# Dealing the rows of a down unit to partitions in neighbouring pairs

## The chip, the cores and the metric

The kernel runs on one core of a Trainium2 chip. The metric is the time of one execution on the device in microseconds; several executions are timed and the median is told. A profiled execution gives the trace.

## The reference

One layer of a decoder for 256 tokens of width 1024, in float32: a mixer (pooling and attention), and then a mixture of experts, which takes nearly all of the time. Of the experts this matters:

```python
for e in range(N_EXPERTS):                       # 32
    gu = jnp.dot(t, w_gu[e]) + b_gu[e]           # t (256, 1024), w_gu[e] (1024, 2048)
    gate = jnp.minimum(gu[:, :D_EXPERT], 7.0)
    lin = jnp.clip(gu[:, D_EXPERT:], -7.0, 7.0)
    act = gate * jax.nn.sigmoid(1.702 * gate) * (lin + 1.0)
    y = jnp.dot(act, w_down[e]) + b_down[e]      # w_down[e] (1024, 1024)
    out = out + combine[:, e:e + 1] * y          # top 4 of 32 experts
```

The weights of the experts are 256 MiB (`w_gu`) and 128 MiB (`w_down`), and each is read once.

## The kernel before

**Units.** The experts' weights come through `raw`, a ring of 12 slots (`RAW`) of 1 MB, each 128 partitions of 8 KB. A unit fills one slot with one DMA. An expert has 8 units of `w_gu` ("gu units") and 4 of `w_down` ("down units"). Gu unit `c` holds the 128 rows `128c` to `128c+127` of `w_gu[e]`, one row of 2048 floats on each partition. Down unit `u` holds the 256 rows `256u` to `256u+255` of `w_down[e]`, two rows of 1024 floats on each partition: partition `p` gets the rows `256u+p` and `256u+128+p`.

**The loading queue.** SyncE issues all units in a fixed order, in `load` (line 296 for gu units, line 302 for down units), after a wait on `unit_used`, which TensorE raises when it has done its last matmul on a unit; so a slot is loaded again as soon as the unit 12 places back is used. The semaphore `raw_loaded` of the slot says that it has landed. The first 12 gu units are issued before the loop over the experts starts.

**TensorE.** The loop runs over pairs of experts, 24 units a pair, 16 pairs. `gu_unit` and `down_unit` multiply up to 64 gathered tokens of the expert by the unit: 8 matmuls of 512 columns each, on the two column halves of the array by turns. In `gu_unit` the tokens lie in `xT`, in `down_unit` in `actT`, and the matmul for block `m = 2u + r` of the hidden channels pairs `actT[:, half, m, :]` with the 1024 floats `raw[:, slot, r*1024:...]`. Partition `p` of block `m` must hold the same hidden channel in both. `mm` is a helper, so all matmuls have line 817.

**From gu to actT.** When the 8 gu units of an expert are done, ScalarE copies the result from PSUM to `gu` (tokens on partitions, line 504), `turn_gu` transposes it in eight 128x128 blocks (line 1035; `gu` is the operand that is loaded as weights or streamed against an identity), VectorE clips both halves (lines 756 and 757) and, with ScalarE's sigmoid (line 509), writes `actT` (line 763). Block `m` of the transpose becomes block `m` of `actT`, channel `128m + p` on partition `p`. Between the units TensorE also does the scatter of the expert before, the gather for the next pair (`gather`), transposes of the dispatch masks (line 1085) and the biases.

**The end.** The last pair's final eight units are all down units; between the second and the third of the last four TensorE does `last_scatter(0)`, after the fourth `last_scatter(1)`; then come the sums into `acc`, the final norm and the store.

Of the kernel before, what the change touches and what calls it, by code (L numbers as in the profile page):

```python
# [25 lines left out]
P = 128  # L26
# [59 lines left out]
def hybrid_layer(nc, x, g_mix, w_in, w_pool, pool_scale, w_out, g_ffn, w_router, b_router,  # L86
                 w_gu, b_gu, w_down, b_down, g_final, consts, out):
    KB = 1024
    with ExitStack() as ctx:
        def sem(name):  # L90
            return ctx.enter_context(nc.semaphore(name))
# [6 lines left out]
        def at(name, shape, dt, off):  # L98
            size = 4
            for s in shape[1:]:  # L100
                size *= s
            assert off + size <= arena_bytes, (name, off, size)
            return nc.alloc_sbuf_tensor_at(name, shape, dt, offset=base + off)

        raw = at("raw", [P, RAW, UW], F32, 0)
        h2 = at("h2", [P, TT, D], F32, 96 * KB)
        gu = at("gu", [P, FE], F32, 128 * KB)
# [97 lines left out]
        def c_(name, rows=P):  # L205
            lo, hi = _AT[name]
            return cst[0:rows, lo:hi]
# [7 lines left out]
        raw_loaded = [sem(f"raw_loaded{s}") for s in range(RAW)]  # L215
# [42 lines left out]
        def pair_of(i):  # L258

            return i % PAIRS  # L260
# [9 lines left out]
        @block.sync  # L270
        def _(sp):
            for t in range(TT):
                sp.dma_start(acc[:, t, :], x[0, t * P:(t + 1) * P, :]).then_inc(x_loaded[t], 16)
            sp.dma_start(cst[:], consts).then_inc(const_loaded, 16)
            for c in range(DC):
                sp.dma_start(raw[:, c, :], w_in[0, c * P:(c + 1) * P, :]).then_inc(raw_loaded[c], 16)
            sp.dma_start(wpool[:], w_pool[0].rearrange("g c d -> c g d")).then_inc(wpool_loaded, 16)
            for b in range(2):
                for h in range(2):
                    sp.dma_start(bgu[b * E:(b + 1) * E, h, :],  # L280
                                 b_gu[0, :, h * FE + b * 512:h * FE + (b + 1) * 512]).then_inc(bgu_loaded, 16)

            sp.dma_start(wout[:], w_out[0].rearrange("(c p) n -> p c n", p=P)).then_inc(wout_loaded, 16)
            sp.dma_start(wrt[:], w_router[0].rearrange("(c p) e -> p c e", p=P)).then_inc(router_loaded, 16)
            sp.dma_start(brt[:], b_router.broadcast_to([P, E])).then_inc(router_loaded, 16)
            sp.dma_start(gffn[:], g_ffn.broadcast_to([P, D])).then_inc(gffn_loaded, 16)
            sp.wait_ge(ysc_zeroed, 1)
            for h in range(2):
                sp.dma_start(ysc[h * SLOTS:h * SLOTS + E, 0, :], b_down[0, :, h * 512:(h + 1) * 512]).then_inc(bdown_loaded, 16)

            def load(e, first, slot_unit):

                s = slot_unit % RAW
                if first < GU_U:
                    src = w_gu[0, bass.ds(e, 1), first * P:(first + 1) * P, :].rearrange("a p n -> p (a n)")
                    sp.dma_start(raw[:, s, :], src).then_inc(raw_loaded[s], 16)  # L296
                else:
                    u = first - GU_U
                    src = w_down[0, bass.ds(e, 1), 2 * u * P:2 * (u + 1) * P, :].rearrange(
                        "a (r p) n -> p (a r) n", p=P)  # L300
                    dst = raw[:, s, :].rearrange("p (r n) -> p r n", r=2)
                    sp.dma_start(dst, src).then_inc(raw_loaded[s], 16)  # L302

            for c in range(PRE_U):
                sp.wait_ge(win_low, c + 1)
                load(0, c, c)
            sp.wait_ge(projected, 3)
            for k in range(EARLY):
                load(1, k, PRE_U + k)
            sp.wait_ge(rounds_ready, 1)  # L310
            last_pair = sp.snap(sp.value_load(further[0:1, 0:1], min_val=0, max_val=T // SLOTS - 1) * PAIRS + (PAIRS - 1))
            sp.dma_start(gfin[:], g_final.rearrange("(a n) -> a n", a=1).broadcast_to([P, D])).then_inc(gfin_loaded, 16)

            def iteration(i, last):
                a = pair_of(i) * 2
                nxt = pair_of(i + 1) * 2
                for k in range(EARLY, ITER_U + (0 if last else EARLY)):
                    if last and k in range(GU_U + DN_U, 2 * GU_U + DN_U):
                        continue
                    at_ = k - (GU_U if last and k >= 2 * GU_U + DN_U else 0)  # L320
                    sp.wait_ge(unit_used, i * ITER_U + PRE_U + at_ - RAW + 1)  # L321
                    if k < GU_U:
                        load(a + 1, k, PRE_U + at_)
                    elif k < GU_U + DN_U:
                        load(a, k, PRE_U + at_)
                    elif k < 2 * GU_U + DN_U:
                        load(nxt, k - GU_U - DN_U, PRE_U + at_)
                    elif k < ITER_U:
                        load(a + 1, k - GU_U - DN_U, PRE_U + at_)
                    else:  # L330
                        load(nxt + 1, k - ITER_U, PRE_U + at_)

            with sp.Fori(0, last_pair) as i:
                iteration(i, False)
            iteration(last_pair, True)

            for t in (1, 0):
                sp.wait_ge(out_ready[t], 1)
                sp.dma_start(out[0, t * P:(t + 1) * P, :], outs[:, t, :]).then_inc(stored, 16)
            sp.wait_ge(stored, 16 * TT)  # L340
# [474 lines left out]
        def _(pe):  # L815
# [27 lines left out]
            def by_channel(c, bank, column):  # L843
                wh, wl = wsp[c % 2][:, 0, :], wsp[c % 2][:, 1, :]
                first, last = c == 0, c == DC - 1
                for j in range(4):
                    o = ps[:, bank + j // 2, (j % 2) * T:(j % 2 + 1) * T]
                    cols = slice(column + j * P, column + (j + 1) * P)
                    mm(o, wh[:, cols], hTh[:, c, :], start=first and j % 2 == 0, stop=False, shared=True)
                    mm(o, wh[:, cols], hTl[:, c, :], start=False, stop=False, shared=True)  # L850
                    ins = mm(o, wl[:, cols], hTh[:, c, :], start=False, stop=last, shared=True)
                return ins
# [11 lines left out]
            for c in range(DC):  # L864
# [3 lines left out]
                u = by_channel(c, 4, 0)  # L868
# [13 lines left out]
            for n, (bank, keys) in enumerate(((0, 2 * P), (4, P))):  # L882
# [3 lines left out]
                for h in range(H):  # L886
                    s = (h % 2) * 4 + h // 2
# [27 lines left out]
            for n in range(6):  # L915
# [6 lines left out]
                for j in range(4):  # L922
                    src = pr0[:, 4 * (n - 4) + j, :] if n >= 4 else pr1[:, 2 * n + j // 2, (j % 2) * P:(j % 2 + 1) * P]
# [107 lines left out]
            def turn_gu(e):  # L1031

                pe.wait_ge(gu_copied, e + 1)
                for m in range(DC):
                    ins = pe.transpose(ps[:, M[m // 4], (m % 4) * P:(m % 4 + 1) * P],  # L1035
                                       gu[:, m * P:(m + 1) * P], c_("ident"))
                ins.then_inc(gu_turned, 1)

            def scatter(t):
# [17 lines left out]
            pe.wait_ge(ysc_zeroed, 2)  # L1057
            pe.wait_ge(dispT_zeroed, 1)
            turn_gu(0)
            pe.wait_ge(rounds_ready, 1)  # L1060
            last_pair = pe.snap(pe.value_load(further[0:1, 0:1], min_val=0, max_val=T // SLOTS - 1) * PAIRS + (PAIRS - 1))

            def iteration(i, last):
# [46 lines left out]
                else:  # L1110
                    pe.wait_ge(dispT_ready, i + 1)
                    pe.wait_ge(gslot_ready, i + 1)
                turn_gu(i * 2 + 1)
                down_unit(0, 2, n_(10), PRE_U + 10)
                down_unit(0, 3, n_(11), PRE_U + 11)
# [9 lines left out]
                for u in range(DN_U):  # L1125
                    down_unit(1, u, n_(20 + u - gap), PRE_U + 20 + u - gap)
                    if u == 1 and not last:
                        pe.wait_ge(gate_clipped, i * 2 + 2)
                        pe.wait_ge(up_clipped, i * 2 + 2)
                        turn_gu(i * 2 + 2)  # L1130
                    if u == 1 and last:
                        pe.wait_ge(outputs_ready, i * 2 + 2)
                        last_scatter(0)
# [35 lines left out]
```

## Time and profile before

| | |
|---|---|
| median of 3 runs | 1087.31 us (1085.9 to 1088.86) |
| the profiled execution, its time | 1088.49 us |
| its span, first to last instruction | 1086.3 us |
| mean granted TensorE clock, share of full speed | 0.994 |
| TensorE matmuls busy | 1022.3 us, 94% of the span |
| VectorE, ScalarE, GpSimd busy | 219.4, 144.7, 21.5 us |
| DMA moved | 419.92 MB in 76933 packets |

Times are microseconds from the first instruction. A line of the profile names the engine (PE is TensorE, PEld its weight load, DVE VectorE, ACT ScalarE, POOL GpSimd, SPq the queue of SyncE), the line of the kernel, the operation with its output and inputs, the shape and how often it ran ("x8"). Matmuls overlap each other, so the stretch that a group covers is shorter than the sum of its parts. The DMA share is the busy share of the core's 16 DMA engines (it can come out a little over 1), GB/s is what they moved.

### The profile page before, as it was taken

How to read it: one execution, taken by the hardware profiler on the slowest of the kernel's cores; microseconds unless marked ns; L12 is line 12 of the kernel's file. 1: busy time of each engine (PE TensorE's matmuls, PEld its weight loads, DVE VectorE, ACT ScalarE, POOL GpSimd, SP SyncE). 2: the span in 40 equal slices, each digit the busy share in tenths (PEclk: the TensorE clock that was granted, in tenths of full speed). 3: DMA queues.
4: the chain of work that ended last, by engine and by line, in shares of the span. 5: the costliest groups of instructions: out<-in, count | busy, mean ns of one | idle time of the engine just before them, and what ended most of it. 6: DMA issues, size and time to landing. Idle time of an engine off the chain costs nothing.

```text
span 1086.3 us, 13772 instructions
## 1 busy us (share of the span) xinstructions
PE 1022.3 (94%) x5165; PEld 420.3 (39%) x5165; DVE 219.4 (20%) x417; ACT 144.7 (13%) x213; POOL 21.5 (2%) x52
## 2 busy tenths in 40 slices
PE   6979999999999998999999998999999998989995
PEld 5956534343434342423334242424233342424231
DVE  4452420212111120211020111201020211202113
ACT  4341311010101010100101010100000010101002
POOL 0030000000000000000000000000000000000000
PEclk9999999999999999999999999999999999999998
DMA  9930599999999999999999999999999999999994
GB/s 378 379 124 1 210 418 400 418 417 418 419 419 419 417 417 417 417 417 417 419 418 419 418 418 417 417 417 416 418 417 418 419 419 417 417 418 416 418 415 187
DMA packets 76933, 419.92 MB, mean 387 GB/s; under 512 B 7717, under 2 KB 8249, under 8 KB 43129
## 3 DMA queue, kind: packets, MB, share of 16 engines
q1 hardware_dynamic: 76880, 419.74, 94.6%
q8 instruction: 9, 0.15, 0.1%
q14 instruction: 4, 0.02, 0.0%
q10 hardware_dynamic: 40, 0.01, 0.0%
HBM read 418.67 MB, written 1.05 MB: 386 GB/s over the span
## 4 chain that ended last, share of the span: by engine, by line
PE 50%; DMA 32%; SPq 14%; DVE 2%; issue 1%; ACT 1%; ACTq 0%; DVEq 0%
PE ps L817 47%; DMA raw<-in_w_gu 29%; SPq L302 7%; SPq L296 6%; DMA raw<-in_w_down 2%; PE ps L1035 1%; PE ps L1085 1%; DMA cst<-in_consts 1%; ACT pr L445 0%; PE ps L924 0%; DVE sm L613 0%; DVE mxs L618 0%; DVE wsp L590 0%; ACT junk L413 0%; SPq L321 0%
## 5 line engine op out<-in xcount | busy, mean ns | idle before, releaser
L817 PE MATMUL ps<-raw,xT 128*64 128x512 f32 x2048 | 470.5, 599 | 14.9 <-DMA raw<-in_w_gu 13.1
L817 PE MATMUL ps<-raw,actT 128*64 128x512 f32 x1024 | 242.1, 601 | 19.0 <-DMA raw<-in_w_down 19.0
L817 PEld LDWEIGHTS ps<-raw,xT 128*64 128x64 f32 x2048 | 134.5, 136 | 318.8 <-issue 251.1
L756 DVE TENSOR_SCALAR gate<-ps 128x512 f32<-128x512 f32 x32 | 22.1, 692 | 556.8 <-PE ps L1035 556.8
L817 PEld LDWEIGHTS ps<-raw,actT 128*64 128x64 f32 x1024 | 65.8, 136 | 158.2 <-issue 98.9
L504 ACT ACTIVATE gu<-ps 128x1024 f32<-128x1024 f32 x32 | 32.8, 1024 | 573.5 <-PE ps L817 573.5
L770 DVE TENSOR_TENSOR acc<-ps,acc 128x512 f32<-128x512 f32 x64 | 41.2, 686 | 163.7 <-PE ps L817 163.7
L817 PE MATMUL ps<-ysc,dispT 64*128 64x512 f32 x272 | 67.8, 615 | 0.9 <-DVE ysc L799 0.9
L817 PEld LDWEIGHTS ps<-disp,h 128*128 128x128 f32 x512 | 60.0, 196 | 13.0 <-issue 12.2
L817 PE MATMUL ps<-disp,h 128*128 128x128 f32 x512 | 63.0, 283 | 0.0
L817 PEld LDWEIGHTS ps<-ysc,dispT 64*128 64x128 f32 x272 | 24.0, 186 | 44.1 <-issue 29.4
L1035 PEld LDWEIGHTS ps<-cst,gu 128*128 128x128 f32 x256 | 27.4, 141 | 27.2 <-issue 27.2
L509 ACT ACTIVATE sig<-gate 128x512 f32<-128x512 f32 x32 | 20.2, 630 | 131.7 <-DVE gate L756 131.7
L817 PE MATMUL ps<-hTh,wsp 128*128 128x256 f32 x192 | 35.9, 283 | 1.6 <-DVE hTl L597 1.6
L1035 PE MATMUL ps<-cst,gu 128*128 128x128 f32 x256 | 35.0, 280 | 1.2 <-ACT gu L504 1.2
L817 PE MATMUL ps<-bgu,sel 32*64 32x512 f32 x256 | 34.8, 613 | 0.0
L817 PE MATMUL ps<-wout,mixT 128*128 128x512 f32 x64 | 30.2, 621 | 3.4 <-ACT mixT L456 3.4
L515 ACT ACTIVATE ysc<-ps,gslot 128x512 f32<-128x512 f32 x31 | 21.3, 687 | 78.4 <-PE ps L817 78.4
L817 PEld LDWEIGHTS ps<-hTh,wsp 128*128 128x128 f32 x192 | 30.5, 192 | 2.1 <-DVE hTl L597 1.8
L497 ACT ACTIVATE xT<-ps 128x512 f32<-128x512 f32 x32 | 19.1, 597 | 65.1 <-PE ps L817 65.1
L817 PE MATMUL ps<-hTl,wsp 128*128 128x256 f32 x96 | 27.2, 283 | 0.0
L380 POOL TENSOR_TENSOR sel<-cst 128x64 f32<-128x64 f32 x32 | 8.8, 294 | 879.1 <-PE ps L817 872.7
(141 smaller groups left out, 396.3 us busy)
## 6 DMA issues: line engine op xcount, KB each, us to landing
raw<-in_w_gu SPq DMA_DIRECT2D x256, 1024.0 KB, 20.6
raw<-in_w_down SPq DMA_DIRECT2D x128, 1024.0 KB, 24.0
raw<-in_w_in SPq DMA_DIRECT2D x8, 1024.0 KB, 15.4
wout<-in_w_out SPq DMA_DIRECT2D x1, 4096.0 KB, 23.6
acc<-in_x SPq DMA_DIRECT2D x2, 512.0 KB, 3.8
out<-outs SPq DMA_DIRECT2D x2, 512.0 KB, 3.1
cst<-in_consts SPq DMA_DIRECT2D x1, 514.0 KB, 6.4
gffn<-in_g_ffn SPq DMA_DIRECT2D x1, 512.0 KB, 5.6
```

The costliest lines, as they stand in the source:

```text
L296: sp.dma_start(raw[:, s, :], src).then_inc(raw_loaded[s], 16)
L302: sp.dma_start(dst, src).then_inc(raw_loaded[s], 16)
L380: pool.tensor_tensor(sel[:, half, :], bc(src, P, SLOTS), c_("ones")[:, 0:SLOTS], ALU.mult).then_inc(sel_ready, 1)
L497: act.activation(xT[:, 4 * job:4 * job + 4].rearrange("p c e s -> p (c e s)"), ps[:, M[job], :], ACT.Copy).then_inc(xT_ready, 1)
L504: act.activation(gu[:], ps[:, GU[half]:GU[half] + 2, :].rearrange("p a b -> p (a b)"), ACT.Copy).then_inc(gu_copied, 1)
L509: act.activation(sig[:], gate[:], ACT.Sigmoid, scale=ALPHA).then_inc(sig_done, 1)
L515: act.activation(ysc[:, half, :], ps[:, Y[half], :], ACT.Copy, scale=gslot[:, half:half + 1]).then_inc(outputs_ready, 1)
L756: dve.tensor_scalar(gate[:], turned[:, :, 0, :], LIMIT, None, ALU.min).then_inc(gate_clipped, 1)
L770: dve.tensor_tensor(part, ps[:, M[job % 2], :], part, ALU.add).then_inc(added, 1)
L817: return pe.matmul(out_, lhsT, rhs, start=start, stop=stop, skip_group_check=shared)
L1035: ins = pe.transpose(ps[:, M[m // 4], (m % 4) * P:(m % 4 + 1) * P], gu[:, m * P:(m + 1) * P], c_("ident"))
L1085: ins = pe.transpose(ps[:, M[0], (2 * a + t) * P:(2 * a + t + 1) * P], disp[:, t, a, :, :].rearrange("p c s -> p (c s)"), c_("ident"))
```

## The change

The DMA of a down unit now gives partition `p` the neighbouring rows `256u+2p` and `256u+2p+1`, which lie one after the other in memory: 8 KB in one run, where there were two runs of 4 KB that lie 512 KB apart. The unit as a whole is the same 1 MB, and its destination is the same slot. So that block `m = 2u + r` of `actT` holds channel `256u + 2p + r` on partition `p`, `turn_gu` reads every second column of `gu` for a block: the 256 columns of blocks `2u` and `2u+1` are dealt to them by turns. Everything else is as before; the number and shapes of all instructions are unchanged.

```diff
@@ load
                     u = first - GU_U
                     src = w_down[0, bass.ds(e, 1), 2 * u * P:2 * (u + 1) * P, :].rearrange(
-                        "a (r p) n -> p (a r) n", p=P)
-                    dst = raw[:, s, :].rearrange("p (r n) -> p r n", r=2)
-                    sp.dma_start(dst, src).then_inc(raw_loaded[s], 16)
+                        "a (p r) n -> p (a r n)", r=2)
+                    sp.dma_start(raw[:, s, :], src).then_inc(raw_loaded[s], 16)
@@ turn_gu
                 for m in range(DC):
                     ins = pe.transpose(ps[:, M[m // 4], (m % 4) * P:(m % 4 + 1) * P],
-                                       gu[:, m * P:(m + 1) * P], c_("ident"))
+                                       gu[:].rearrange("p (u q r) -> p u r q", q=P, r=2)[:, m // 2, m % 2, :], c_("ident"))
```

## Rows read from the trace of the kernel before

**Rows 1.** The page: TensorE's and the DMA engines' busy tenths in 40 slices, packets.

```profile
PE   6979999999999998999999998999999998989995
PEclk9999999999999999999999999999999999999998
DMA  9930599999999999999999999999999999999994
...
DMA packets 76933, 419.92 MB, mean 387 GB/s; under 512 B 7717, under 2 KB 8249, under 8 KB 43129
```

**Rows 2.** The chain that ended last, in order of time: start, us, what.

```profile
175.28 21.92 PE ps L817 x104
...
231.10 21.92 PE ps L817 x104
...
355.30 18.05 DMA raw<-in_w_gu
373.40 9.52 PE ps L817 x40
...
415.53 18.06 DMA raw<-in_w_gu
...
475.77 18.05 DMA raw<-in_w_gu
...
1036.00 9.55 PE ps L817 x40
1046.93 19.25 DMA raw<-in_w_down
1066.22 7.46 PE ps L817 x32
```

**Rows 3.** Windows: stretch, us, clock, DMA share, GB/s; 8 us among down units, 18 among gu units.

```profile
446.00:454.00 8.00, 1.00 1.03 411
456.00:474.00 18.00, 1.00 1.02 423
...
807.40:815.40 8.00, 1.00 1.02 408
817.40:835.40 18.00, 1.00 1.02 424
...
988.20:996.20 8.00, 1.00 1.02 409
998.20:1016.20 18.00, 1.00 1.02 423
```

**Rows 4.** Packets by stretch: down units 416:424, gu units 426:444, `wout` 32:34, 34:36, 36:38.

```profile
DMA packets 848, 3.29 MB, mean 411 GB/s; under 512 B 52, under 2 KB 52, under 8 KB 842
DMA packets 1056, 7.60 MB, mean 422 GB/s; under 512 B 119, under 2 KB 119, under 8 KB 137
DMA packets 202, 0.83 MB, mean 414 GB/s; under 512 B 0, under 2 KB 0, under 8 KB 202
DMA packets 198, 0.81 MB, mean 406 GB/s; under 512 B 0, under 2 KB 0, under 8 KB 198
DMA packets 203, 0.83 MB, mean 416 GB/s; under 512 B 0, under 2 KB 0, under 8 KB 203
```

**Rows 5.** Timeline, weight loads that waited for a unit to land: start, us, what [idle <-releaser].

```profile
476.18 0.20 PEld L817 LDWEIGHTS ps<-raw,xT 128*64 128x64 f32 x4 [1.42 <-DMA raw<-in_w_gu]
478.67 0.20 PEld L817 LDWEIGHTS ps<-raw,xT 128*64 128x64 f32 x4 [1.43 <-DMA raw<-in_w_gu]
481.23 0.20 PEld L817 LDWEIGHTS ps<-raw,actT 128*64 128x64 f32 x4 [1.50 <-DMA raw<-in_w_down]
483.79 0.20 PEld L817 LDWEIGHTS ps<-raw,actT 128*64 128x64 f32 x4 [1.50 <-DMA raw<-in_w_down]
```

**Rows 6.** Timeline of TensorE: a turn, matmuls of one unit, a gather.

```profile
459.17 1.09 PE L1035 MATMUL ps<-cst,gu 128*128 128x128 f32 x8
...
441.21 1.94 PE L817 MATMUL ps<-raw,xT 128*64 128x512 f32 x8
...
453.54 3.84 PE L817 MATMUL ps<-disp,h 128*128 128x128 f32 x32
```

**Rows 7.** Timeline of SyncE's queue: the first issues after the start, then early and late ones.

```profile
131.87 5.37 SPq L296 DMA_DIRECT2D raw<-in_w_gu  x4
...
168.79 10.62 SPq L302 DMA_DIRECT2D raw<-in_w_down  x4
...
440.49 13.94 SPq L296 DMA_DIRECT2D raw<-in_w_gu  x8
454.68 16.49 SPq L302 DMA_DIRECT2D raw<-in_w_down  x4
```

**Rows 8.** Issue to landing: first units (131 to 139), down units of 168.7 to 180.

```profile
DMA to landing us min/median/max: 4.7/6.4/8.0
DMA to landing us min/median/max: 6.0/6.5/9.3
```

## The prediction

> **What bounds the kernel now.** I read the page's slices first, then the chain in order of time, then windows over single stretches. The slices show two resources that both look full: TensorE is busy nine tenths or more nearly everywhere, and so are the DMA engines from the fifth slice to the last but one [rows 1]. Only the rhythm tells which of them sets the pace. In the first pairs the chain runs through TensorE, and the same piece comes back after 231.10 - 175.28 = 55.82 us: that is a pair when TensorE is the limit. From about 355 us on the chain runs through landings of gu units, and the period is 475.77 - 415.53 = 60.24 us: that is a pair when the loads are the limit [rows 2]. In between nothing changed but the stock of loaded slots: TensorE had 12 units in hand at the start and used them up. So from the first issue after the start, at 131.87 us [rows 7], to the end, the loads run without a break, and the kernel ends when they end. TensorE has a reserve: the piece at 373.40 comes back at 1036.00, 11 periods later, and at each of them TensorE alone would have needed 60.24 - 55.82 = 4.42 us less. That is 11 x 4.42 = 48.6 us that TensorE spends waiting.
>
> The second thing to see is that the loads have two speeds. In stretches in which only gu units move, the windows show 422 to 423 GB/s, in stretches in which only down units move 409 to 411 (sometimes 408), both at a DMA share of 1.02 or 1.03: the engines are as busy, but move less [rows 3]. There are 21 such pairs of windows between 416 and 1056 us; their means are 409.4 and 422.5 GB/s; the pair with 408 and 424 is the one furthest apart. The packet counts say what differs: among down units nearly all packets (842 - 52 = 790 of 796) are under 8 KB, among gu units nearly none (18 of 937) [rows 4]. A unit of 1048576 bytes therefore takes 1048576 / 409.4 = 2.561 us as a down unit and 1048576 / 422.5 = 2.482 us as a gu unit.
>
> The landings say the same in another way. Where TensorE waits for each unit, gu units follow each other after 478.67 - 476.18 = 2.49 us and down units after 483.79 - 481.23 = 2.56 us [rows 5]. As a check, 16 x 2.482 + 8 x 2.561 = 60.20 us, and the chain's period is 60.24 [rows 2].
>
> **The change, part by part.**
>
> *The DMA of a down unit.* It takes on exactly the form of a gu unit's DMA: 128 partitions, one run of 8 KB each, 1 MB in one piece of memory. The nearest row for it is the gu stretch [rows 3], and I take its speed: 2.561 - 2.482 = 0.079 us less for each down unit. There are 128 of them. The last two don't count: the chain enters TensorE for the last time at 1066.22, after the landing of the second of the last four, and from there on it is 7.46 us of TensorE's own work (`last_scatter(0)` stands before the third unit), so the last two units have landed when they are wanted [rows 2]. So 126 x 0.079 = 10.0 us. The bounds: by the landings the difference is 2.56 - 2.49 = 0.07, which gives 8.8 us. By the fastest gu and the slowest down window (424 and 408 GB/s) it is 2.570 - 2.473 = 0.097, which gives 12.2 us. I stay with 10.0, because it is the mean over 21 pairs of windows.
>
> *Does it count from the first unit?* In the first pairs the chain is TensorE's [rows 2], so a faster load gives nothing there at once. It fills the ring faster, and the stock lasts longer: the loads become the limit later, and the gain comes out then. That holds while the DMA engines always have work. The thinnest place is near 170 to 180 us, where down units take 6.0 us from issue to landing, against 4.7 us for the quickest of the first units, which had hardly anything ahead of it [rows 8]. Up to there only 8 down units have become faster, 8 x 0.079 = 0.6 us, and the margin is 6.0 - 4.7 = 1.3 us. I take nothing off.
>
> *SyncE's queue.* A down unit's issue takes 10.62 us for four while slots are scarce, and 16.49 us for four, 13.94 us for eight gu units, once the ring is full; the second is the queue pushing back, since a whole pair's issues add up to the period [rows 7]. Half the runs in a down unit means less pushing back, and SyncE may issue earlier. With the DMA engines full this moves no landing. I cost it at nothing, and expect the chain to show less of SyncE.
>
> *The turns.* Eight transposes per expert, 256 in all, read `gu` with a step of two floats. Today a turn of eight covers 1.09 us, with 0.27 of it the tail of the last, so 0.117 us per transpose [rows 6]. The trace has no operand of TensorE with a step between single floats; the nearest is the gather, which reads its mask in two runs of 64 with a gap and needs 3.84 / 32 = 0.12 us for each, no more [rows 6]. Bounds: nothing from below (a step can't read faster than no step), and from above I take half the rate as what a step of two could well cost, 0.117 us more each, 16 x 0.117 = 1.9 us per pair (a loss beyond that is the third rival). The reserve per pair after the change is 60.24 - 8 x 0.079 - 55.82 = 3.79 us, so even half the rate is hidden; only the first turns' latency would show, and that runs beside two down units, whose matmuls take 1.94 us each. I take nothing. If TensorE had no reserve, half the rate would cost 256 x 0.117 = 30 us.
>
> **The sum.** The profiled execution has 1088.49 us; 1088.49 - 10.0 = 1078.5. It stands 1.18 us above the median of the runs, so against the median the forecast is 1087.31 - 10.0 = 1077.3 us. A pair should then take 60.24 - 0.63 = 59.61 us.
>
> **The rivals.**
>
> *Only a part of the difference goes with the length of the runs.* The rest would be the place of `w_down` in memory. The trace has one more transfer in runs of 4 KB, `wout`: the last 2 us of its stretch show 416 GB/s [rows 4]. By it a unit in 4 KB runs takes 2.521 us, only 0.039 more than a gu unit, and the gain is 126 x 0.039 = 4.9 us: 1082.4. Against it: the 4 us before show 414 and 406 GB/s, so that the three together have 412, and all 21 down windows are slow by the same amount. A page speaks for this rival. The Trainium skill, "DMA: Bandwidth & Descriptors", section "Why small descriptors are slow (HBM only)", gives a fixed overhead of about 3 cycles per packet beside one cycle for 32 bytes, and holds that joining descriptors is worth it only up to 256 bytes. By its figures (an estimate) two runs of 4 KB cost 262 cycles and one of 8 KB 259, 1.15% of a down unit's time, some 3.7 us in all; the windows' 3.1% are more than that, so the trace does not agree.
>
> *No change.* Either the whole difference belongs to `w_down` and not to the runs, or the DMA is still cut at 4 KB. Then 1087.3. For it: nothing in the rows; no transfer of `w_down` in 8 KB runs is there to look at. Against it: `wout` in 4 KB runs is slower than the gu stretches too, and gu units show that 8 KB packets exist [rows 4].
>
> *TensorE becomes the limit: slower.* If a read with a step of two floats ran at a quarter of the rate, each transpose would take 3 x 0.117 = 0.35 us more, 256 of them 90 us. The reserve of 48.6 us covers the first part; what is left is 1087.3 + 90 - 48.6 = 1128.7 us. This rival begins to eat the gain at (48.6 - 10) / 256 = 0.15 us per transpose and makes the kernel slower than before from 48.6 / 256 = 0.19 us. For it: no row excludes it. Against it: it needs more than half the rate lost. The Trainium skill, "SBUF — State Buffer", says that memory is read in lines of 16 bytes and that two hits on a line are enough for full speed; a step of two floats gives two. By that the turns cost nothing; no row here shows it.
>
> **How the numbers follow.** What a measurement of this kernel can tell from no change is about 0.3%, 3.3 us. Chances: forecast 0.80, own range 1074 to 1080 (8.8 to 12.2 us of gain, and some 1 us for the spread of the runs); a part only 0.10, at 1082 to 1084; no change 0.06; slower by TensorE 0.04. The range from 1074 to 1082.5 takes in the first case and half of the second. Faster by over 0.3% (below 1084.0) holds the first two, less a little of the second's edge: 0.88. Within 0.3%: 0.08. Slower: 0.04.
>
> **What would show it.** Windows among down units go from 409 to 422 GB/s, and the period in the chain's later part to 59.6 us. The packets under 8 KB fall by 32768 from 43129, and all packets by 16384 from 76933. Landings of down units follow after 2.49 us. The turn stays at 1.09 us; at 2 us or more the reserve shrinks, at some 3 us it is gone. The prediction is wrong if down windows stay near 409 with 8 KB packets (then it is the place in memory), if the gu windows fall as the down windows rise (then something common to both holds the pace), or if TensorE's turn grows by more than 1.2 us.

## The result and the profile after

The changed kernel takes 1079.18 us (median of 6 runs, 1078.48 to 1079.78), the kernel before 1087.14 us (median of 6, 1085.9 to 1088.86). The ratio is 0.9924, with a 95% interval of 0.9913 to 0.9934: 8.0 us less, between 7.2 and 9.5. The forecast was 1077.3 us, 10 us less. The profiled execution of the changed kernel took 1079.25 us, with a span of 1077.1 us. The span is 9.2 us shorter than the one of before, more than the medians say, because the profiled execution of before lies 1.35 us above its median and this one on it.

The page of the changed kernel, its slices and its packets, to be read against [rows 1]:

```profile
PE   6979999999999999999999999999999999999995
DMA  9930499999999999999999999999999999999994
GB/s 377 375 137 1 198 418 399 423 423 422 422 422 422 422 422 422 422 422 422 422 422 422 422 422 422 421 422 422 422 422 422 422 422 422 422 421 422 422 421 187
DMA packets 60548, 419.92 MB, mean 390 GB/s; under 512 B 7716, under 2 KB 8248, under 8 KB 10360
```

The same bytes go in 16385 packets fewer, and 32769 fewer are under 8 KB: each down unit's 256 runs of 4 KB have become 128 of 8 KB (128 units, so 16384 and 32768; the one packet more belongs to another queue). From the eighth slice to the last but one the rate is 421 to 423 GB/s. The two speeds are gone.

The chain that ended last, of the changed kernel, in order of time (start, us, what), beside [rows 2]:

```profile
231.26 21.92 PE ps L816 x104
...
287.35 21.92 PE ps L816 x104
...
407.90 22.76 DMA raw<-in_w_gu
430.71 9.52 PE ps L816 x40
...
490.35 9.52 PE ps L816 x40
...
967.55 9.52 PE ps L816 x40
...
1029.17 27.78 DMA raw<-in_w_down
```

While TensorE sets the pace a pair takes 287.35 - 231.26 = 56.09 us, 0.27 more than before. Where the loads set it, the piece at 430.71 comes back nine periods later at 967.55: 536.84 / 9 = 59.65 us, 0.59 less than before. The chain enters its first landing of a gu unit at 407.90 us, where it was 355.30: TensorE's stock of loaded slots lasts longer.

Two more things of the changed kernel, in the timeline: the waits for down units near the end (TensorE's weight loads, [idle <-releaser]), beside [rows 5], and a turn, beside [rows 6].

```profile
1054.51 0.20 PEld L816 LDWEIGHTS ps<-raw,actT 128*64 128x64 f32 x4 [1.43 <-DMA raw<-in_w_down]
1057.00 0.20 PEld L816 LDWEIGHTS ps<-raw,actT 128*64 128x64 f32 x4 [1.43 <-DMA raw<-in_w_down]
...
1048.93 1.23 PE L1034 MATMUL ps<-cst,gu 128*128 128x128 f32 x8
```

Down units now follow each other after 1057.00 - 1054.51 = 2.49 us, where it was 2.56. The turn of eight has grown from 1.09 to 1.23 us.

SyncE's queue in the changed kernel, beside [rows 7]:

```profile
168.55 10.71 SPq L301 DMA_DIRECT2D raw<-in_w_down  x4
...
600.86 8.46 SPq L301 DMA_DIRECT2D raw<-in_w_down  x4
609.79 19.41 SPq L296 DMA_DIRECT2D raw<-in_w_gu  x8
```

In the later part four down issues take 8.46 to 10.71 us, not 16.49, and the page gives SyncE's queue 0% of the chain, where it had 14%. The issues go out earlier, the landings don't follow: by the pages the median time from issue to landing of a gu unit has grown from 20.6 to 25.0 us.

### The profile page after: what moved, and what is told of

Read it like the earlier page. It is cut to its first block, busy times and chain, and to the rows that moved or that the text cites. A ratio compares the mean times of both kernels' runs of the same rounds, so it can differ in the third digit from the quotient of the medians.

```text
span 1077.1 us, 13772 instructions
## 1 busy us (share of the span) xinstructions
PE 1023.2 (95%) x5165; PEld 426.6 (40%) x5165; DVE 219.4 (20%) x417; ACT 144.7 (13%) x213; POOL 21.4 (2%) x52
## 2 busy tenths in 40 slices
DMA packets 60548, 419.92 MB, mean 390 GB/s; under 512 B 7716, under 2 KB 8248, under 8 KB 10360
## 4 chain that ended last, share of the span: by engine, by line
PE 68%; DMA 28%; DVE 2%; ACT 1%; issue 0%; SPq 0%; ACTq 0%; DVEq 0%
PE ps L816 65%; DMA raw<-in_w_gu 25%; DMA raw<-in_w_down 3%; PE ps L1034 2%; PE ps L1084 1%; DMA cst<-in_consts 1%; ACT pr L444 0%; PE ps L923 0%; DVE sm L612 0%; DVE mxs L617 0%; DVE wsp L589 0%; ACT junk L412 0%; DVE outs L807 0%; ACT wsp L421 0%; PE ps L960 0%
## 5 line engine op out<-in xcount | busy, mean ns | idle before, releaser
L1034 PEld LDWEIGHTS ps<-cst,gu 128*128 128x128 f32 x256 | 33.2, 209 | 27.2 <-issue 27.2
L1034 PE MATMUL ps<-cst,gu 128*128 128x128 f32 x256 | 39.2, 296 | 1.2 <-ACT gu L503 1.2
```

## The experiments

Eleven kernels were run. Each was timed in turns with the kernel before on the same chip, and each ratio is to that.

### The two parts of the change by themselves

`dma_alone` is the changed kernel with the old turns, `turns_alone` the kernel before with the new ones (each leaves out the other half of the pairing, so its output is not the layer's):

```diff
@@ dma_alone, against the changed kernel
-                                       gu[:].rearrange("p (u q r) -> p u r q", q=P, r=2)[:, m // 2, m % 2, :], c_("ident"))
+                                       gu[:, m * P:(m + 1) * P], c_("ident"))
@@ turns_alone, against the kernel before
-                                       gu[:, m * P:(m + 1) * P], c_("ident"))
+                                       gu[:].rearrange("p (u q r) -> p u r q", q=P, r=2)[:, m // 2, m % 2, :], c_("ident"))
```

> The kernel after with the turns put back to neighbouring columns, so that only the down units' DMA differs from before; hidden channels are paired with the wrong rows of w_down, so the output is not the layer's. If the whole gain comes from the loads and the turns are hidden behind them: 1079 us, ratio 0.992 to 0.993, the same as the changed kernel. If the slower turns of the changed kernel (weight load 209 ns, not 141) take part of the gain back: up to 256 x 0.017 = 4 us less, 1075 us, ratio 0.989.

Measured: 1078.39 us, ratio 0.9918 (0.9904 to 0.9931).

> The kernel before with only the turns changed to every second column; hidden channels are paired with the wrong rows of w_down, so the output is not the layer's. If the turns are hidden: 1087 us, ratio 0.999 to 1.001, a pair of experts still 60.24 us in the later part and some 0.27 us more (56.09) in the first pairs. If they lie on the path: 1087 + 4 = 1091 us, ratio 1.004.

Measured: 1087.99 us, ratio 1.0004 (0.9995 to 1.0013). The whole gain comes with the loads. Whether the turns take 0.8 us of it (1079.18 against 1078.39) can't be told: the intervals overlap.

### Length of the runs, or the distance between them

The change makes the runs longer and also brings a partition's two rows together. `near_4k_split` has neighbouring rows and yet runs of 4 KB, with two DMAs for each down unit. `far_4k_split` is its control, the rows of before, also with two DMAs.

```diff
@@ load, near_4k_split, against the changed kernel
                     src = w_down[0, bass.ds(e, 1), 2 * u * P:2 * (u + 1) * P, :].rearrange(
-                        "a (p r) n -> p (a r n)", r=2)
-                    sp.dma_start(raw[:, s, :], src).then_inc(raw_loaded[s], 16)
+                        "a (p r) n -> p (a r) n", r=2)
+                    for r in range(2):
+                        sp.dma_start(raw[:, s, r * D:(r + 1) * D], src[:, r, :]).then_inc(raw_loaded[s], 16)
@@ load, far_4k_split, against the kernel before
-                    dst = raw[:, s, :].rearrange("p (r n) -> p r n", r=2)
-                    sp.dma_start(dst, src).then_inc(raw_loaded[s], 16)
+                    for r in range(2):
+                        sp.dma_start(raw[:, s, r * D:(r + 1) * D], src[:, r, :]).then_inc(raw_loaded[s], 16)
```

(In both, TensorE waits for both DMAs of a down unit, 32 and not 16 on its semaphore.)

> Neighbouring rows as in the changed kernel, but in runs of 4 KB: each down unit is loaded by two DMAs of 512 KB, one for the even rows and one for the odd. If the length of a run sets the pace: a down unit still takes 2.56 us, windows of down units show 409 GB/s, time 1087 us (ratio 0.999 to 1.002) plus what the two DMAs cost in far_4k_split. If it is the 512 KB between the two rows of a partition: 2.48 us, 422 GB/s, 1079 us, ratio 0.993.

> The control for near_4k_split: the rows of the kernel before (p and p + 128), also with two DMAs of 512 KB for each down unit, each of them one piece of memory. If a DMA by itself costs nothing where the engines are full: 1087 us, ratio 0.999 to 1.001. Run length: the same time as near_4k_split within 0.1%. Distance: since each DMA now reads one piece of 512 KB, 1079 us here too, ratio 0.993.

Measured: `near_4k_split` 1087.58 us, ratio 1.0002 (0.9992 to 1.0011); `far_4k_split` 1087.18 us, ratio 1.0000 (0.9991 to 1.0009). Two windows of `near_4k_split`, the first among down units, the second among gu units (stretch, us, clock, DMA share, GB/s):

```profile
446.00:454.00 8.00, 1.00 1.03 410
456.00:474.00 18.00, 1.00 1.01 422
```

With the rows together and the runs short, nothing is gained: the distance is not it. Nor does a second DMA for the same bytes cost anything that can be measured.

### The same on the other tensor

`gu_4k` is the kernel before with the gu units cut as well: two neighbouring units exchange a half. The first of them holds the gate half of row `p` and the lin half of the row 128 further on, the second holds the other two halves.

```diff
@@ load; gu_unit
-                    src = w_gu[0, bass.ds(e, 1), first * P:(first + 1) * P, :].rearrange("a p n -> p (a n)")
-                    sp.dma_start(raw[:, s, :], src).then_inc(raw_loaded[s], 16)
+                    dst = raw[:, s, :].rearrange("p (r n) -> p r n", r=2)
+                    if first % 2 == 0:
+                        lo = (first * P - 1) * 2 * FE if first else 0
+                        q0 = 2 if first else 0
+                        flat = w_gu[0, bass.ds(e, 1), :, :].rearrange("a k n -> a (k n)")
+                        src = flat[:, lo:lo + 2 * 257 * FE].rearrange("a (r q n) -> q (a r) n", r=2, q=257)[q0:q0 + 2 * P - 1:2]
+                    else:
+                        lo = (first - 1) * P * 2 * FE + FE
+                        flat = w_gu[0, bass.ds(e, 1), :, :].rearrange("a k n -> a (k n)")
+                        src = flat[:, lo:lo + 2 * 255 * FE].rearrange("a (r q n) -> q (a r) n", r=2, q=255)[0:255:2]
+                    sp.dma_start(dst, src).then_inc(raw_loaded[s], 16)
...
-                        col = h * FE + b * 512
-                        ins = mm(ps[h * SLOTS:(h + 1) * SLOTS, GU[half] + b, :], xT[:, c, half, :],
+                        col = (h + c) % 2 * FE + b * 512
+                        ins = mm(ps[h * SLOTS:(h + 1) * SLOTS, GU[half] + b, :], xT[:, c + h * (1 - 2 * (c % 2)), half, :],
```

> The kernel before, with the gu units in runs of 4 KB too: two neighbouring gu units exchange a half, so that each partition gets 4 KB of one row and 4 KB of the row 128 further on; the same matmuls in the same order. If the run length sets the pace on any tensor: a gu unit rises from 2.48 to 2.56 us, a pair takes 24 x 2.561 = 61.5 us, the time is 1087 + 244 x 0.079 = 1106 us, ratio 1.018. If the slowness of down units belongs to w_down or its place in memory: 1087 us, ratio 1.000.

Measured: 1105.48 us, ratio 1.0163 (1.0146 to 1.0180). Chain of `gu_4k` (start, us, what), one landing per pair:

```profile
893.84 18.32 DMA raw<-in_w_gu
955.28 18.32 DMA raw<-in_w_gu
```

A pair takes 61.44 us, so a unit in runs of 4 KB takes 61.44 / 24 = 2.560 us, on either tensor. The rival that left a part of the difference to `w_down` is out.

### Shorter and longer runs

`far_2k` cuts the down units of before into runs of 2 KB. `down_16k` loads down units of the changed kernel in twos, four neighbouring rows on a partition. `all_16k` does so with gu units too, two neighbouring rows on a partition.

```diff
@@ load, far_2k, against the kernel before; down_unit reads col = h * D + r * 512
-                        "a (r p) n -> p (a r) n", p=P)
-                    dst = raw[:, s, :].rearrange("p (r n) -> p r n", r=2)
+                        "a (r p) (h n) -> p (a h) r n", p=P, h=2)
+                    dst = raw[:, s, :].rearrange("p (h r n) -> p h r n", h=2, r=2)
@@ load, down_16k and all_16k, against the changed kernel; the odd unit of two issues nothing
+                        src = w_down[0, bass.ds(e, 1), 2 * u * P:2 * (u + 2) * P, :].rearrange(
+                            "a (p r) n -> p (a r n)", r=4)
+                        sp.dma_start(raw[:, s:s + 2, :].rearrange("p s n -> p (s n)"), src).then_inc(raw_loaded[s], 16)
@@ turn_gu, both
+                                       gu[:].rearrange("p (u q r) -> p u r q", q=P, r=4)[:, m // 4, m % 4, :], c_("ident"))
@@ load and gather, all_16k
+                        src = w_gu[0, bass.ds(e, 1), first * P:(first + 2) * P, :].rearrange(
+                            "a (p r) n -> p (a r n)", r=2)
...
+                        h2[:, t, :].rearrange("p (w q r) -> p w r q", q=P, r=2)[:, c // 2, c % 2, :]
```

> The kernel before with down units in runs of 2 KB (the two rows of a partition are laid out in halves by turns): 32 runs for each DMA engine in a unit, not 16. If each run costs the same fixed time, (2.561 - 2.482) / 8 = 0.0099 us per engine: a down unit takes 2.561 + 16 x 0.0099 = 2.72 us, 386 GB/s, and the time is 1087 + 126 x 0.158 = 1107 us, ratio 1.018. If only runs over some size are favoured and 4 KB and 2 KB are alike: 1087 us.

Measured: 1106.14 us, ratio 1.0173 (1.0156 to 1.0190).

> The kernel after with down units loaded two at a time, by one DMA of 2 MB with one run of 16 KB per partition (four neighbouring rows); the turns read every fourth column. If the fixed time per run holds further: 4 runs per engine and MB, a unit 2.482 - 4 x 0.0099 = 2.442 us, 429 GB/s, 126 x 0.040 = 5.0 us saved and 1.9 us lost at the end, where TensorE gets the last but two units together: 1076 us, ratio 0.990. If 8 KB is already the ceiling or runs are cut at 8 KB: 1081 us, ratio 0.9945.

Measured: 1077.25 us, ratio 0.9903 (0.9887 to 0.9920).

> As down_16k, and the gu units also two at a time in runs of 16 KB (two neighbouring rows); the gather reads every second column of h2. If the fixed time per run holds further: a pair of experts 24 x 2.442 = 58.6 us, 372 x 0.040 = 14.9 us saved and 1.9 lost: 1066 us, ratio 0.981. If 8 KB is the ceiling or runs are cut there: 1081 us, ratio 0.9945. If TensorE becomes the limit by its strided reads (over 58.6 - 56.1 = 2.5 us more per pair): above 1066 with no waits for loads in the later pairs.

Measured: 1070.58 us, ratio 0.9845 (0.9828 to 0.9861). One landing per pair, or per two pairs, from the chains of the three (start, us, what), `far_2k` first:

```profile
950.11 22.48 DMA raw<-in_w_gu
...
1011.56 22.50 DMA raw<-in_w_gu
```

```profile
484.49 25.80 DMA raw<-in_w_down
...
603.15 25.80 DMA raw<-in_w_down
```

```profile
877.09 21.60 DMA raw<-in_w_gu
935.80 21.62 DMA raw<-in_w_gu
```

Pairs take 61.45 us, 118.66 / 2 = 59.33 us and 58.71 us (58.73 as a mean over five pairs of `all_16k`). With 2.485 us for a unit in 8 KB runs (59.65 / 24, the changed kernel), a down unit in 2 KB runs takes (61.45 - 16 x 2.485) / 8 = 2.711 us; a unit in 16 KB runs takes 58.71 / 24 = 2.446 us, and by `down_16k` (59.33 - 16 x 2.485) / 8 = 2.446 us as well.

The runs per DMA engine are counted as if the 16 engines share a unit's runs evenly.

| run | runs per DMA engine and MB | us per MB | GB/s | ns per run saved on the way from the row above |
|---|---|---|---|---|
| 2 KB | 32 | 2.711 | 387 | |
| 4 KB | 16 | 2.560 | 410 | 9.4 |
| 8 KB | 8 | 2.485 | 422 | 9.4 |
| 16 KB | 4 | 2.446 | 429 | 9.8 |

Each run costs a DMA engine about the same, 9.4 to 9.8 ns, at lengths from 2 to 16 KB. That runs of 16 KB were not cut into shorter ones is seen in the packets of `all_16k`:

```profile
DMA packets 32900, 419.91 MB, mean 393 GB/s; under 512 B 4644, under 2 KB 5176, under 8 KB 7288
```

Against the changed kernel these are 60548 - 32900 = 27648 fewer: 24576 for the 384 units, each with 64 runs where it had 128, and 7716 - 4644 = 3072 packets under 512 B, 16 for each of the 192 DMAs that are gone.

`all_16k` kept less than was expected of it, 1070.6 against 1066 us. The 1066 already had a loss of 1.9 us at the end in it, and the end costs about that: from TensorE's last wait for a unit to the end of the span it needs 1068.4 - 1046.62 = 21.8 us, the changed kernel 1077.1 - 1057.00 = 20.1. `all_16k_tail` loads the last four down units one by one:

```diff
@@ load, all_16k_tail, against all_16k, for the last four down units; TensorE waits for each
+                    src = w_down[0, bass.ds(e, 1), (u - u % 2) * 2 * P:(u - u % 2 + 2) * 2 * P, :].rearrange(
+                        "a (p x r) n -> p x (a r n)", x=2, r=2)[:, u % 2, :]
+                    sp.dma_start(raw[:, s, :], src).then_inc(raw_loaded[s], 16)
```

> all_16k, with the last four down units loaded one by one in runs of 8 KB. If the 1.7 us between TensorE's last wait and the end (21.8 us against 20.1 in the changed kernel) comes from the last units landing two by two: 1.5 us less than all_16k less 0.2 us for the 8 KB runs, 1069 us, ratio 0.983. If the loads' end sets it anyhow: as all_16k, 1070.6 us, ratio 0.9845.

Measured: 1068.35 us, ratio 0.9826 (0.9809 to 0.9842), the fastest kernel of this study, 10.8 us under the changed one. The two intervals overlap, but its slowest execution (1069.40) is below the fastest of `all_16k` (1069.83). So the last units' landing two by two costs some 2 us.

Most of what `all_16k` lost beyond its forecast, some 4.5 us, lies at the start. Windows of `all_16k` and then of the changed kernel show how the stream fills (stretch, us, clock, DMA share, GB/s):

```profile
130.00:140.00 10.00, 1.00 0.62 229
...
170.00:180.00 10.00, 1.00 0.96 378
180.00:190.00 10.00, 1.00 0.98 369
```

```profile
130.00:140.00 10.00, 1.00 0.70 274
...
170.00:180.00 10.00, 1.00 0.99 394
180.00:190.00 10.00, 1.00 1.00 389
```

A DMA that needs two free slots starts later (the first issue after the start at 132.87 us, against 131.59), and near 175 us, where the prediction had found the thinnest place, the engines are less full (0.96 and 0.98, against 0.99 and 1.00). In these three windows `all_16k` moves (45 + 16 + 20) GB/s x 10 us = 0.81 MB less, 2 us of work. The forecast also counted a gain for each of the some 21 units that move before 190 us, 21 x 0.04 = 0.8 us, which they can't have had, and its 0.040 us per unit was 0.039, 0.4 us in all. A little over 1 us was not traced, and no run removed any of this.

### TensorE with the cover taken away

`half_load` is the kernel before with loads that can't be the limit, `half_load_turns` the same with the new turns.

```diff
@@ load, half_load, after the first 12 units
-                    sp.dma_start(raw[:, s, :], src).then_inc(raw_loaded[s], 16)
+                    sp.dma_start(raw[:, s, 0:FE], src[:, 0:FE]).then_inc(raw_loaded[s], 16)
...
-                    src = w_down[0, bass.ds(e, 1), 2 * u * P:2 * (u + 1) * P, :].rearrange(
-                        "a (r p) n -> p (a r) n", p=P)
+                    src = w_down[0, bass.ds(e, 1), 2 * u * P:(2 * u + 1) * P, :].rearrange("a p n -> p (a n)")
+                    sp.dma_start(raw[:, s, 0:D], src).then_inc(raw_loaded[s], 16)
```

> The kernel before, but after the first 12 units each unit loads only half of its slot (the first 4 KB of each partition), so that loads can't be the limit; the other half of a slot holds old data and the output is not the layer's. It measures TensorE's reserve by itself. If the reserve is what the prediction worked out from the chain (4.42 us for each of 11 pairs, 48.6 us): 1087.3 - 48.6 = 1039 us, ratio 0.955, a pair of experts 55.82 us to the end. If loads and matmuls slow each other down: below 1030 us.

Measured: 1035.20 us, ratio 0.9520 (0.9504 to 0.9536).

> half_load with the turns reading every second column, as in the changed kernel: the price of the turns when nothing hides them. By the first pairs of the changed kernel (56.09 us against 55.82) 16 x 0.27 = 4.3 us more than half_load: 1043 us, ratio 0.959. If the prediction's bound of half the rate holds: 16 x 1.9 = 30 us more. If nothing: 1039 us.

Measured: 1039.13 us, ratio 0.9558 (0.9542 to 0.9574). The chains of the two (start, us, what), `half_load` first:

```profile
788.77 21.92 PE ps L818 x104
...
844.60 21.92 PE ps L818 x104
```

```profile
790.74 21.92 PE ps L818 x104
...
846.83 21.92 PE ps L818 x104
```

A pair takes 55.83 us without and 56.09 us with the new turns. With nothing to hide them all 256 transposes together cost 3.9 us, 0.015 us each.

## Why the prediction was right, and where its sizes were off

**What bounds the kernel.** Right. TensorE is busy 94% of the span and is not the limit: with the loads halved the same work ends at 1035.2 us. The reserve was put at 48.6 us and is 1087.5 - 1035.2 = 52.3 us (1087.5 is the kernel before, timed beside `half_load`). The sum took 11 whole periods and left out what comes before the first and after the last of them.

**The load.** The mechanism was right: a down unit takes on the speed of a gu unit, and the length of the runs decides, neither the distance between them nor the tensor (`near_4k_split`, `gu_4k`). The size was a little too big. The term was 2.561 - 2.482 = 0.079 us per down unit; by whole periods it is 2.560 - 2.485 = 0.075 us. The 4 KB side was right. The 8 KB side was read from windows inside the gu stretches, which show 422.5 GB/s; the changed kernel, where every unit is in 8 KB runs, moves 1048576 / 2.485, which is 422.0. 126 x 0.075 = 9.4 us then stands for the 10.0, at the edge of the measured 7.2 to 9.5. In the two traces, from the first issue after the start to TensorE's last wait, the stream has become 934.35 - 925.41 = 8.94 us shorter (131.87 to 1066.22, and 131.59 to 1057.00). The 0.5 us between 9.4 and 8.94 is that of the first eight down units ("From which unit it counts", below). `dma_alone`, with the same loads, is 9.4 us below its kernel before by the medians and 8.9 us by the ratio, so the 8.0 us of the changed kernel's medians need no other cause than the spread of the runs.

**The price of a run.** From 4 to 8 KB the rate rises by 3.0%, from 8 to 16 KB by 1.6%. The Trainium skill, "DMA: Bandwidth & Descriptors", section "Why small descriptors are slow (HBM only)", gives an overhead of about 3 cycles per packet and holds that putting consecutive descriptors together is worth it only up to 256 bytes. The runs here do not agree: by the prediction's estimate from that page of the Trainium skill a down unit would have gained 1.15%, and it gained 0.075 of 2.560 us, 2.9%. Another section of that page of the Trainium skill, "Where 436 GB/s comes from", gives 435.2 GB/s as what the ports can take. With this the table agrees, by an extrapolation: taking 9.4 ns for each of the 8 runs from 2.485 us leaves 2.41 us per MB, 435 GB/s.

**From which unit it counts.** Right in the main: TensorE sets the pace in the first pairs, and the saved time comes out later. Wrong for the first eight down units, from which the prediction took nothing off. Windows of the kernel before and then of the changed one (stretch, us, clock, DMA share, GB/s):

```profile
134.00:194.00 60.00, 1.00 1.01 411
194.00:254.00 60.00, 1.00 1.02 418
```

```profile
134.00:194.00 60.00, 1.00 1.01 410
194.00:254.00 60.00, 1.00 1.01 422
```

Until 194 us the changed kernel moves no more than the kernel before, although eight down units have shorter loads by then. From 170 to 190 us both move under 400 GB/s, 391 and 392, less than at either of the two speeds, and SyncE issues the next units at the same times in both to 0.3 us (168.79 and 168.55, 181.94 and 181.83): there the slots that TensorE frees set the pace of the loads. So the margin of 1.3 us, which the prediction took from issue-to-landing times, was not there, and 118 down units count: 118 x 0.075 = 8.85 us, against the 8.94 of the two traces.

**SyncE's queue.** Right: four down issues take 8.46 to 10.71 us in place of 16.49, and the landings did not come earlier. The share of the chain, 14% before and 0% after, is a weak sign of it: `turns_alone`, whose down units are loaded as before and whose issues still take up to 16.50 us for four, has 1%.

**The turns.** Costed at nothing, and they cost nothing that can be measured (`turns_alone`). The bound of 1.9 us per pair was far above the real price, 56.09 - 55.83 = 0.26 us. The weight load of one block has gone from 141 to 209 ns, as the rows of each line's instructions show, before, after and in `all_16k`:

```profile
L1035 PEld LDWEIGHTS ps<-cst,gu x256: 138/141/143, 144.8 to 1058.6; 128*128 128x128 f32 x128
```

```profile
L1034 PEld LDWEIGHTS ps<-cst,gu x256: 194/209/222, 144.5 to 1049.8; 128*128 128x128 f32 x128
```

```profile
L1050 PEld LDWEIGHTS ps<-cst,gu x256: 195/212/220, 144.1 to 1041.2; 128*128 128x128 f32 x128
```

(min, median and max in ns.) Only 0.015 us of these 0.07 us reach the path when nothing else hides them. Weight loads run beside matmuls: 420.3 us of the one and 1022.3 us of the other lie in a span of 1086.3 us.

The step has no such price everywhere. In `all_16k` the gather reads its weights, `h2`, with a step of two floats as well, and its weight loads of the same shape take about what they took (medians 192 and 196 ns). The pages of the kernel before and of `all_16k` (busy us, mean ns):

```profile
L817 PEld LDWEIGHTS ps<-disp,h 128*128 128x128 f32 x512 | 60.0, 196 | 13.0 <-issue 12.2
```

```profile
L830 PEld LDWEIGHTS ps<-disp,h 128*128 128x128 f32 x512 | 61.5, 196 | 13.0 <-issue 12.2
```

These loads need some 195 ns from neighbouring columns too. Why the transposes' loads start from 141 ns and these don't, no run shows.

**The rivals.** "Only a part" and the first form of "no change" needed the difference to sit in `w_down`; `gu_4k` shows that it doesn't. The second form, a DMA still cut at 4 KB, is out by the packets: 10360 under 8 KB, where there were 43129. "TensorE becomes the limit" needed 0.19 us per transpose; it is 0.015.

## What to carry to other kernels

Where the loads set the pace, look at how the bytes are cut before looking at how many there are: here windows over stretches with one kind of transfer showed two rates at the same busy share, and the runs found a fixed cost per run behind it. Count only the transfers that the loads pace: while another engine frees the slots, a faster load gains nothing. Which rows go to which partition is free wherever the sum over channels doesn't care for their order, as long as the other operand is dealt the same way; the price of that dealing is then an operand read with a step, and whether it shows depends on the reserve of the engine that reads it. Longer loads saved time per byte, but they need more free slots at once and land late at the end, where keeping the last ones short gave 2.2 us back.

## What the runs showed of the hardware

- A run costs a DMA engine 9.4 to 9.8 ns beside its bytes, about the same at 2, 4, 8 and 16 KB. Splitting a unit's DMA in two, with the same runs, costs nothing while the engines are full (`near_4k_split` and `far_4k_split`: pair 60.24 and 60.23 us, where it was 60.24, ratio 1.0002 and 1.0000), although each DMA brings 16 packets under 512 B with it (9764 of them, against 7716 in the changed kernel). These small packets are not such runs.
- TensorE loads the 128x128 float32 blocks of the turns as weights in 141 ns from neighbouring columns, in 209 ns from every second and in 212 ns from every fourth: one step up, and the step of four costs hardly more than that of two. The Trainium skill, "SBUF — State Buffer", section "Specifications (TRN2)", says that two hits on a line of 16 bytes are enough for full speed. For the turns' weight loads the runs don't agree: every second float gives two hits and is slower, every fourth gives one and is the same. For the gather's weight loads they do: a mean of 196 ns from neighbouring columns and 196 ns from every second.
